# Convolution Silus in pairs, and rotary angles behind the first gated norm

## The reference

```python
zxbcdt = rms_norm(h, norm_w) @ in_w
z, xbc, dt = split(zxbcdt, [2048, 2048 + 3072])
xbc = silu(conv4(xbc) + conv_b)                    # causal, width 4, by channel
xs, bm, cm = split(xbc, [2048, 2048 + 512])
y = ssd_chunked(xs, softplus(dt + dt_bias), -exp(a_log), bm, cm)   # 4 chunks of 128
y = (y + d_skip * xs) * silu(z)
y = y * rsqrt(mean(y * y over the 512 columns of a group) + eps) * gnorm_w
h = h + y @ out_w
...
ang = positions * inv_freq                         # rope, used only in the second layer
cos, sin = cos(ang), sin(ang)
```

## Time and profile before

| | |
|---|---|
| median of the three timed executions | 1388.23 us |
| the profiled execution, its own time | 1387.61 us |
| its span (first to last instruction) | 1385.1 us |
| PE busy | 1350.1 us, 97% |
| DVE busy | 831.0 us, 60% |
| ACT busy | 677.9 us, 49% |
| POOL busy | 525.6 us, 38% |
| granted TensorE clock | 0.995 of full, 9 in all of the 40 slices |

### The profile page before, as it was taken

How to read it: one execution, slowest core, us unless ns; L and a number is a source line. 1 busy time by engine, 2 the same in 40 slices (tenths; PEclk the granted TensorE clock), 3 DMA queues, 4 the chain that set the end, 5 groups by cost and what they waited for, 6 DMA issues and landing times.

```text
span 1385.1 us, 17824 instructions
## 1 busy us (share of the span) xinstructions
PE 1350.1 (97%) x6628; PEld 1062.1 (77%) x6628; DVE 831.0 (60%) x1417; ACT 677.9 (49%) x1130; POOL 525.6 (38%) x259
## 2 busy tenths in 40 slices
PE   9989999999999999999999999999999999999997
PEld 6867778777688878767888887766667888888886
DVE  6775554757567744785677323477755645544666
ACT  7664635636466533784565312355545332232463
POOL 3553544636220134466000344136433655555200
PEclk9999999999999999999999999999999999999999
DMA  5221222222123232211233232130012232332331
GB/s 196 94 74 47 92 70 83 77 72 77 65 97 102 77 92 93 63 44 55 99 91 122 97 135 87 37 116 16 17 46 76 94 104 91 97 101 92 122 107 61
DMA packets 33796, 116.93 MB, mean 84 GB/s; under 512 B 4140, under 2 KB 4652, under 8 KB 33456
## 3 DMA queue, kind: packets, MB, share of 16 engines
q1 hardware_dynamic: 32408, 111.62, 25.1%
q10 hardware_dynamic: 1304, 4.19, 0.8%
HBM read 113.70 MB, written 2.10 MB: 84 GB/s over the span
## 4 chain that ended last, share of the span: by engine, by line
PE 88%; DVE 5%; ACT 3%; issue 2%; DMA 1%; POOL 1%; ACTq 0%; DVEq 0%
PE bank L1306 85%; PE bank L1762 1%; PE bank L1604 1%; DMA h<-in_xT 0%; ACT wsh L864 0%; DVE arena L1957 0%; POOL arena L773 0%; DVE arena L2037 0%; PE bank L1480 0%; PE bank L1515 0%; DMA ring<-in_wstream 0%; DVE wsl L1843 0%; DVE arena L2329 0%; DVE ssacc L1838 0%; DVE arena L2243 0%
## 5 line engine op out<-in xcount | busy, mean ns | idle before, releaser
L710 POOL TENSOR_TENSOR wsl<-ring,wsh 128x1024 fp32r<-128x1024 f32 x143 | 348.8, 2440 | 543.6 <-ACT wsh L864 543.4
L864 ACT ACTIVATE wsh<-ring 128x1024 fp32r<-128x1024 f32 x196 | 207.2, 1058 | 452.8 <-PE bank L1306 429.9
L1306 PE MATMUL bank<-parts1h,wsh 128*128 128x512 f32 (+1 forms) x736 | 292.8, 398 | 6.1 <-POOL wsl L710 2.2
L1306 PE MATMUL bank<-parts1h,wsl 128*128 128x512 f32 (+1 forms) x736 | 285.6, 388 | 0.0
L1306 PE MATMUL bank<-parts1l,wsh 128*128 128x512 f32 (+1 forms) x736 | 285.6, 388 | 0.0
L1306 PE MATMUL bank<-parts0h,wsh 128*128 128x512 f32 x696 | 277.8, 399 | 3.8 <-issue 1.3
L1306 PE MATMUL bank<-parts0h,wsl 128*128 128x512 f32 x696 | 271.3, 390 | 0.0
L1306 PE MATMUL bank<-parts0l,wsh 128*128 128x512 f32 x696 | 271.1, 390 | 0.0
L1306 PEld LDWEIGHTS bank<-parts1h,wsh 128*128 128x128 f32 x736 | 138.6, 188 | 43.1 <-issue 9.7
L1306 PEld LDWEIGHTS bank<-parts0h,wsh 128*128 128x128 f32 x696 | 130.7, 188 | 40.9 <-issue 10.8
L1306 PEld LDWEIGHTS bank<-parts1l,wsh 128*128 128x128 f32 x736 | 138.8, 189 | 28.8 <-issue 2.2
(11 more groups left out here) (322 smaller groups left out, 1802.7 us busy)
## 6 DMA issues: line engine op xcount, KB each, us to landing
ring<-in_wstream SPq DMA_DIRECT2D x204, 512.0 KB, 3.5
arena<-in_alibi ACTq DMA_DIRECT2D x2, 1024.0 KB, 5.1
outT<-arena SPq DMA_DIRECT2D x8, 256.0 KB, 2.8
h<-in_xT SPq DMA_DIRECT2D x4, 256.0 KB, 6.3
h<-in_xT ACTq DMA_DIRECT2D x4, 256.0 KB, 5.8
ring<-in_wstream SPq DMA_DIRECT2D x2, 256.0 KB, 4.5
arena<-in_frow ACTq DMA_DIRECT2D x1, 512.0 KB, 3.4
arena<-in_cmpb ACTq DMA_DIRECT2D x1, 496.0 KB
```

Source lines behind the costliest of these rows:

```text
L710: return nc.gpsimd.tensor_tensor(dst, src, hi.bitcast(F32), ALU.subtract)
L864: nc.scalar.activation(wsh[n % NSET][:, :], src, ACT.Copy).then_inc(*done("high", ("high", L)))
L1306: return nc.tensor.matmul(*args, **kw)
```

## The change

There are four edits.

1. Scalar program: `silu_open` (one Silu) becomes `silus`, which issues all Silus that are open. It is called at the beginning of a projection step, ahead of the weight split's copy, when two are open or the step is one with i of 6 to 9, and at "ssd0" as before. It is no longer called behind the first tap.
2. At such a call in a group g of 1 to 3 with i < 6, a one-column Exp is issued behind the Silus, which fetches the Exp table, and ACT waits for its end.
3. "angles" moves from behind ssd0 of group 0 to behind "gb" of group 0.
4. "sines" moves from behind the fourth ssd1 of group 0 to behind proj (1, 9), which is the last step before ssd0 of group 1.

```diff
--- before.py
+++ after.py
@@ -157,15 +157,12 @@
         k = 0
         for i, x in enumerate(scan):
             out.append(x)
-            if x == ("ssd0", 0):
-                out.append(("angles",))
-            if x == ("ssd1", 0, 3):
-                out.append(("sines",))
             while k < len(fill) and k * len(scan) < (i + 1) * len(fill):
                 out.append(fill[k])
                 k += 1
         out += fill[k:]
-        out += [("yt", g, m) for m in range(GT)] + head[:1] + [("ya", g)] + head[1:] + [("gn", g)] + mid + [("gb", g)] + tail
+        out += [("yt", g, m) for m in range(GT)] + head[:1] + [("ya", g)] + head[1:] + [("gn", g)] + mid + [("gb", g)]
+        out += [("angles",)] + tail + [("sines",)] if g == 0 else tail
     def early(name, m):
         return [("he", name, m)]
 
@@ -828,10 +825,9 @@
 
             conv_open = []
 
-            def silu_open():
-
-                if conv_open:
-                    g, i = conv_open.pop()
+            def silus():
+
+                for g, i in conv_open:
                     act.wait_ge(*at("conv", g, i))
                     if g >= 2:
 
@@ -842,10 +838,15 @@
                     dst = bcT[g % 2][:, i, :] if i < 2 else xs[g % 2][:, i - 2, :]
                     nc.scalar.activation(dst, cva[(g * 6 + i) % 2], ACT.Silu)\
                         .then_inc(*done("silu", ("xbc", g, i), ("conv_used", g * 6 + i)))
+                conv_open.clear()
 
             for number, step in enumerate(STEPS):
                 (hnh, hnl), (xgh, xgl) = roles(number)
                 k, a = step[0], step[1:]
+                if k == "proj" and (len(conv_open) == 2 or a[1] >= 6):
+                    silus()
+                    if a[0] and a[1] < 6:
+                        link(nc.scalar.activation(tiny[:, :], eps[:, :], ACT.Exp))
                 if k == "ple" and a[1]:
                     square(2 * a[0] + 2 if a[0] < 2 else 7, a[1] - 1)
                 for b, n in splits_at(step):
@@ -962,10 +963,8 @@
                         nc.scalar.activation(cva[n % 2], b[:, :], ACT.Identity, bias=vec[:, V_CB + ch:V_CB + ch + 1],
                                              scale=vec[:, V_CW + 3 * 24 + ch:V_CW + 3 * 24 + ch + 1])\
                             .then_inc(*done("conv0", ("conv0", g, i)))
-                        silu_open()
                         conv_open.append((g, i))
                     else:
-                        silu_open()
                         if g >= 1:
                             act.wait_ge(*at("ygated", g - 1, i - 6))
                         nc.scalar.activation(zs[:, i - 6, :], b[:, :], ACT.Silu)\
```

## The result

| | before | after |
|---|---|---|
| median of the timed executions, us | 1388.42 (6: 1386.51 to 1390.50) | 1395.70 (6: 1394.05 to 1398.11) |
| profiled execution, its own time / span, us | 1387.61 / 1385.1 | 1395.95 / 1394.1 |
| mean granted clock of the profiled execution | 0.995 | 0.993 |

The change makes the kernel 7.3 us slower: ratio 1.0056, 95% interval 1.0042 to 1.0069. The forecast was slower, 1393.0 us (+4.8), range 1389.5 to 1396.5. All engines' instructions are the same but for ACT's, which has 11 more.

What follows compares the result with a forecast made beforehand. PE, busy 1350.1 of 1385.1 us, was taken to bound the kernel, so only its order of waits matters. Terms 4.8 + 0.8 - 0.8 + 0 = +4.8 us gave 1393.0 us, range 1389.5 to 1396.5.

Steps and rivals of the forecast that it cites:

- the two heads: First two gated norms, around proj (1,6) and (2,6): Silus and a table load delay the weight split, PE waits 2.4 us each.
- rival D: Worse: work ahead of the splits and the angles collide with POOL, tap delays go through in full; 1396.0 us, chance 0.13.
- A: The forecast itself: the summed terms hold, 1393.0 us; chance 0.62.
- Part 1: Silus ahead of the split at proj (g+1, 6): 2 x 2.4 = +4.8 us for groups 0 and 1, nothing for group 2.
- The third head: Gated norm around proj (3,6), behind group 2: Silus fall into an idle gap behind an earlier-issued split; nothing counted.
- Part 2: Silus ahead of the split at proj (0,2) and (0,4) wait for DVE's taps, making PE late: +0.8 us, +0.2 to +1.0.
- Part 3: Silus and table loads taken out of the scans: DVE's idle 1.34 us in group 2 go; -0.8 us, bounds 0 and -1.3.
- Part 4: Table loads counted: 6 more, 7.7 us more of ACT; all but those at the first two gated norms fall into gaps.
- Part 5: Angles and sines at their new places fit DVE's idle time and ACT's gap: 0 us, up to 1 us without cover.
- B: The heads cost less: table loads run ahead of the squares, each head 1.1 us, sum +2.2; 1390.4 us, chance 0.17.
- C: Faster: ACT's table switching holds the scan up, fewer switches let DVE run ahead; -4.5 us, 1383.7 us, chance 0.08.

Runs made afterwards that it cites:

- number 5: Changed kernel with the Silus put behind the split's copy again only at the first two gated norms, proj (1,6) and (2,6): ratio to before 1.0007.
- number 2: Changed kernel with the Silus put behind the split's copy again at all three gated norms (steps with i of 6 to 9): ratio to before 1.0059.
- number 6: Changed kernel with the Silus behind the split's copy at the first two gated norms and group 0's Silus in the old order: ratio to before 0.9998.
- number 8: Changed kernel without the one-column Exp that fetches Exp's table behind the Silus: ratio to before 1.0024.
- number 1: Kernel before with only edits 3 and 4, angles and sines moved: ratio to before 1.0004.
- number 3: Changed kernel with group 0's Silus in the old order, one behind each first tap: ratio to before 1.0062.
- number 4: Changed kernel with the Silus behind the split's copy at all three gated norms and group 0's Silus in the old order: ratio to before 1.0046.
- number 9: Changed kernel with the Silus put behind the split's copy at proj (1,6) alone: ratio to before 1.0030.
- number 10: Changed kernel with the Silus put behind the split's copy at proj (2,6) alone: ratio to before 1.0036.
- number 7: Kernel before with ACT's first tap ahead of the split's copy at projections with i below 6: ratio 0.9970, 1383.29 us.
- number 11: Changed kernel with the first two gated norms and group 0 repaired, and the first tap ahead of the split's copy: ratio 0.9963, 1381.86 us.

## Why the prediction was right, and where it was not

**Direction and mechanism.** Right, and for the reason given: the two heads. Waits cost 4.6 to 5.8 us by span x clock (1384.5 against the three sets of before, 5.4 against the first), where the sum was 4.8. The measured 7.3 us have a second cause that is in no term of the sum, the clock. (5.4 and the clock's 3 are more than 7.3, since the sets of before differ by 1 us in each of the two.) That the total lies in the range is in part luck: +7.3 is above the sum's own upper bound of +6.8. The range reaches to 1396.5 on account of rival D, and the measured 1395.70 is nearer to D's 1396.0 than to A's 1393.0, but what fills the gap is the clock and not what D names.

**Part 1, the heads, +4.8.** The copy is late by 3.01 - 0.54 = 2.47 us. PE's waits on POOL are 2.54 us and 2.27 us, where before no idle time was shown at either place. Together 4.8 us; number 5 measures 5.4 in span x clock, with executions' noise. The third head cost nothing, as said; number 2 shows why the Silus belong ahead of the copy there.

**Part 2, +0.8.** PE waited 0.58 us by the idle figure, and its start slipped from 70.83 to 72.43. Of that, 0.78 us comes from the first 20 us of the span, ahead of every place that was changed (cb's matmuls in front began at 70.36 instead of 69.58); the other 0.82 us is part 2. Numbers 5 and 6 give 0.96, within their noise. ACT's timeline shows the steps, to be held against the earlier trace rows:

```profile
53.47 0.63 ACT L839 ACTIVATE arena<-arena 128x512 f32<-128x512 f32 x1 [1.05 <-DVE arena L1956]
...
68.26 0.63 ACT L839 ACTIVATE arena<-arena 128x512 f32<-128x512 f32 x1 [4.85 <-DVE arena L1956]
68.79 1.04 ACT L865 ACTIVATE wsh<-ring 128x1024 fp32r<-128x1024 f32 x1
```

Less the 0.78 us, Silu (0,1) starts at 52.69 (the working had 52.66 + 0.07), the copy at (0,4) at 68.01 (67.32 to 68.15) and PE at 71.65 (70.98 to 71.81): each step as worked out.

**Part 3, -0.8.** Wrong in its sign: +0.2. The idle 1.34 us of DVE did go, and the first of the two waits fell from 0.53 to 0.20; but the second rose from 0.47 to 1.04. DVE's timeline there:

```profile
272.26 2.08 DVE L2021 SCALAR_TENSOR_TENSOR arena<-arena 128x1024 f32<-128x1024 f32 x1
...
277.09 2.57 DVE L1979 TENSOR_TENSOR parts1h<-parts1l,con 64x1024 fp32r<-64x1024 f32 x1
279.58 2.06 DVE L2021 SCALAR_TENSOR_TENSOR arena<-arena 128x1024 f32<-128x1024 f32 x1
```

L2021 takes 2.08 us instead of 1.23, since it now meets POOL's multiplication, and L1979, which in the trace of before took 2.00 beside POOL's split, 2.57 (POOL's runs from 276.16 to 278.58). What DVE won by starting earlier it lost by running beside POOL. The prediction named this and gave it half of the gain; it took more than all. The bound of 0 excluded a loss, which was the mistake. The second wait grew by 0.57 us, and so did L1979. One reading of the prediction was off as well: in the trace of before the Silu and the first of the two loads (260.26 and 258.97) stand ahead of the Relu at 260.80, and only the second load (261.88) between Relu and Exp. All are in front of the Exp, so the argument stands.

**Part 4, loads.** Counted right for Silu (11) and the fetch (6), and for the 3 that Exp loses; but the whole is 5 loads more and not 6, since the sines' own load went too (below). With the 6 one-column activations these are ACT's 11 additional instructions. Groups of ACT, 40 to 350 us:

```profile
L839 ACT ACT_TABLE_LOAD x11 | 14.1, 1283 | 0.2
...
L849 ACT ACT_TABLE_LOAD x6 | 7.7, 1283 | 0.1
```

These loads in ACT's idle time cost nothing that numbers 5 and 6 can tell. The rule of the Trainium skill, page "ScalarE: Activation LUTs", section "Table sets: the hidden batching unit", to do all of one set before switching, was put with rival C, by which the change would have won; the runs don't bear it out here (ratio 1.0056 for the change, 0.9998 for number 6). In these runs a switch mattered only where PE waits for what is behind it, and the fetch that was to hide one load made another one visible (number 8).

**Part 5, angles and sines, 0.** Right. DVE's timeline:

```profile
156.74 1.25 DVE L2140 CAST small<-pos 128x4 f32<-128x4 int32 x1
158.01 2.44 DVE L2143 TENSOR_TENSOR arena<-small,rowb 128x128 f32<-128x128 f32 x1
160.49 0.23 DVE L2145 TENSOR_SCALAR arena<-arena 128x128 f32<-128x128 f32 x1
```

and ACT's:

```profile
157.29 0.58 ACT L970 ACTIVATE arena<-bank 128x512 f32<-128x512 f32 x1
162.58 0.31 ACT L1067 ACTIVATE arena<-arena 128x128 f32<-128x128 f32 x1 [4.71 <-DVE arena L2155]
```

The nine instructions take 5.8 us (156.74 to 162.54) instead of 2.6, the first two 1.25 and 2.44 us beside POOL; ACT waits 4.71 us. POOL's split runs from 157.92 to 160.31, the second of the nine from 158.01 to 160.45. Still number 1 measures 1.0004. One detail was wrong: no load stands between the gate's Silu (157.29) and the sines, so one table served both.

**The clock, +3, not in the sum.** Its part was 9.1 us in the change's executions, 5.4 to 6.5 in those of before. In the profile of the change the two spells behind PE's waits cost 3.4 us x half = 1.7 us each, which is PE's 3.1 us of additional busy time but for 0.3; and 3 us is about what lay between the forecast's +4.8 and the result's +7.3. The prediction took the clock from a row of before that said 1.00 and didn't ask what the new waits would do to it. This is the step that the sum lacks: a price for the clock behind each new wait. A single profile doesn't give that price. The old wait of 1.96 us is the same in before, in the change and in numbers 1 to 6 and 8 to 10; a spell stands behind it in seven of these eleven profiles (the change, numbers 1 to 6) and none in the other four (before, numbers 8, 9 and 10). In the two kernels in which it is halved, 7 and 11, there is none. What decides between the seven and the four stays open. Over many executions there is an order, though: the clock's part is 9.1 to 12.0 us in the four kernels with both heads' waits or the 4.05 us wait (the change and numbers 2 to 4), 7.8 and 8.3 in the two with one head's wait, and 5.0 to 7.3 in all others. Numbers 2 to 4 were measured beside a set of before with 5.9. So new long waits do cost clock on average; how much of the change's own 3 us is theirs and how much chance stays open, since the sets of before spread over 1 us and the change's has 6 executions.

**Rivals.** B (a load ahead of the squares) is out by ACT's timeline: the load comes behind the fourth square. C (switching holds the scan up) is out by numbers 5, 6 and 11. D (collisions with POOL) was right that DVE and the angles collide with POOL, and wrong about the price.

## What to carry to other kernels

Where PE starts a block as soon as its weights are ready, what is put ahead of the weights' preparation is paid by PE (here a copy 2.47 us late cost waits of 2.54 and 2.27 us); ask of every place whether the consumer waits for this copy or for a later one (head 3 wanted the opposite of heads 1 and 2). A fetched table is only worth something if nobody needs the old table before the idle time ends (here the fetch cost 1.4 us at each of two heads). A new wait of PE can also cost clock: forecast it, or say that it is left out. And to shorten the wait for a PSUM bank, move what frees the bank ahead of what has slack: here that one exchange was worth 4.5 us, while pairing and fetching gained nothing.

## What the runs showed of the hardware

- Behind some waits of PE of 1.96 to 4.06 us TensorE ran at 1.2 instead of 2.4 GHz for some 3.4 us (at the 4.06 us wait of number 2 for some 6.6, from within the wait on), which costs 1.7 us where PE is busy; behind others it did not. In the change's profile the waits of 1.96 and 2.54 us had such a spell and that of 2.27 us had none. The same wait of 1.96 us had one in number 1 and none in before.
- DVE instructions of 0.3 to 0.5 us can take as long as a whole POOL instruction beside them: 2.44 us for a 128x128 TENSOR_TENSOR that took 0.29 in before (POOL's split took 2.39), 2.47 us for a 64x512 TENSOR_SCALAR that otherwise takes 0.49.
- A table load started before its activation's wait was over the earlier trace rows, but at the first gated norm not ahead of the square in front of it (square at 136.86 for 0.63 us, load at 137.51).
